# The third unit of each up projection waits for all four PSUM tiles of its opening

## What is computed

```
def swiglu_ffn(x, w_in, w_down):                      # layers 0 and 1
    h = x @ w_in                                      # 1024 -> 2 * 2816
    g, u = h[..., :FFN_HIDDEN], h[..., FFN_HIDDEN:]
    return (jax.nn.silu(g) * u) @ w_down

def _conv_ffn(h, w_up, conv_w, conv_b, w_down):       # second block
    a = h @ w_up
    ap = jnp.pad(a, ((0, 0), (CONV_W - 1, 0), (0, 0)))
    conv = conv_b + ap[:, 0:S] * conv_w[0]
    for j in range(1, CONV_W):
        conv = conv + ap[:, j:j + S] * conv_w[j]
    gate, val = jnp.split(conv, 2, axis=-1)
    return (jax.nn.silu(gate) * val) @ w_down
```

## Time and profile before

| | |
|---|---|
| median of 3 runs | 2296.75 us |
| all runs | 2290.5, 2296.75, 2320.01 us |
| span of the profiled execution | 2302.4 us |
| TensorE busy | 2235.3 us, 97% |
| VectorE busy | 1271.0 us, 55% |
| ScalarE busy | 936.0 us, 41% |
| mean granted TensorE clock | 0.994 of full |

### The profile page before, as it was taken

The page is one execution under the profiler, slowest core; times in us unless marked ns, Lnnn a source line. Parts: engine busy times, 40 slices in busy tenths (PEclk is TensorE's granted clock), DMA queues, the critical chain, the costliest instruction groups (busy, mean ns, idle before and its releaser), DMA issues.

```text
span 2302.4 us, 47528 instructions
## 1 busy us (share of the span) xinstructions
PE 2235.3 (97%) x18842; PEld 2140.7 (93%) x18846; DVE 1271.0 (55%) x2590; ACT 936.0 (41%) x1547; POOL 298.9 (13%) x318
## 2 busy tenths in 40 slices
PE   7999999999999999989999999999999998999998
PEld 7978999999999996978999999999989898999998
DVE  6477443665553256889463476554165655656513
ACT  4566354332222143478363252222144554444312
POOL 3000300200000052336120110000033002000001
PEclk9999999999999999999999999999999999999999
DMA  6333341255542221200252245553312202333221
GB/s 172 81 94 92 104 143 56 83 140 142 138 137 101 91 66 56 74 2 1 92 164 75 74 110 140 154 144 110 106 49 92 79 20 75 91 104 97 95 106 55
DMA packets 303947, 219.07 MB, mean 95 GB/s; under 512 B 34442, under 2 KB 290384, under 8 KB 303824
## 3 DMA queue, kind: packets, MB, share of 16 engines
q1 hardware_dynamic: 251856, 188.79, 27.4%
q10 hardware_dynamic: 50208, 25.69, 4.3%
q0 software_dynamic: 1760, 2.88, 0.4%
HBM read 207.58 MB, written 2.10 MB: 91 GB/s over the span
## 4 chain that ended last, share of the span: by engine, by line
PE 90%; ACT 4%; DVE 2%; POOL 2%; issue 1%; DMA 0%; DVEq 0%; SPq 0%; POOLq 0%; ACTq 0%
PE bank L714 69%; PE bank L831 5%; PE bank L940 4%; PE bank L910 2%; PE bank L1259 2%; PE bank L1039 1%; PE bank L1210 1%; PE bank L1108 1%; POOL ZS L2562 1%; PE bank L1100 1%; PE bank L1193 1%; ACT SQ L1559 1%; PE bank L1311 1%; ACT BI L1355 1%; POOL ZS L2531 1%
## 5 line engine op out<-in xcount | busy, mean ns | idle before, releaser
L714 PE MATMUL bank<-XH,WH 128*128 128x256 f32 (+1 forms) x3184 | 887.4, 279 | 6.2 <-DVE HF L2245 2.7
L714 PE MATMUL bank<-XH,WL 128*128 128x256 f32 (+1 forms) x3184 | 886.0, 278 | 0.0
L714 PE MATMUL bank<-XL,WH 128*128 128x256 f32 (+1 forms) x3184 | 886.0, 278 | 0.0
L681 DVE TENSOR_TENSOR WL<-RAW,WH 128x2048 fp32r<-128x2048 f32 x160 | 369.4, 2309 | 521.5 <-ACT WH L677 521.5
L714 PEld LDWEIGHTS bank<-XH,WH 128*128 128x128 f32 (+1 forms) x3184 | 599.0, 188 | 7.1 <-issue 4.1
L714 PEld LDWEIGHTS bank<-XH,WL 128*128 128x128 f32 (+1 forms) x3184 | 600.5, 189 | 0.0
L714 PEld LDWEIGHTS bank<-XL,WH 128*128 128x128 f32 (+1 forms) x3184 | 597.4, 188 | 0.2 <-issue 0.2
L677 ACT ACTIVATE WH<-RAW 128x2048 fp32r<-128x2048 f32 x171 | 327.5, 1915 | 584.1 <-PE bank L714 545.6
L714 PE MATMUL bank<-HH,WH 128*128 (+1 forms) x1056 | 293.4, 278 | 0.9 <-DVE HF L2245 0.9
L714 PE MATMUL bank<-HH,WL 128*128 (+1 forms) x1056 | 293.3, 278 | 0.0
L714 PE MATMUL bank<-HL,WH 128*128 (+1 forms) x1056 | 293.2, 278 | 0.0
(11 more groups left out here) (359 smaller groups left out, 3666.6 us busy)
## 6 DMA issues: line engine op xcount, KB each, us to landing
RAW<-in_ffn_w_in SPq DMA_DIRECT2D x88, 512.0 KB, 4.7
MB<-in_mod_w ACTq DMA_DIRECT2D x48, 512.0 KB, 5.0
RAW<-in_ffn_w_down SPq DMA_DIRECT2D x44, 512.0 KB, 4.0
RAW<-in_ffn_up SPq DMA_DIRECT2D x44, 512.0 KB, 4.6
RAW<-in_xa_w_kv SPq DMA_DIRECT2D x32, 512.0 KB, 4.4
RAW<-in_ffn_down SPq DMA_DIRECT2D x22, 512.0 KB, 3.9
RAW<-in_xa_w_q SPq DMA_DIRECT2D x16, 512.0 KB, 4.2
RAW<-in_xa_w_o SPq DMA_DIRECT2D x16, 512.0 KB, 4.0
```

What stands on the lines that cost most here:

```text
L681: nc.vector.tensor_tensor(WL[:, par, :], RAW[:, par, :], f32(WH[:, par, :]), ALU.subtract).then_inc(w_split, 1)
L714: mm = nc.tensor.matmul(out_ap[:, cols], l, moving, start=(start and n == 0 and k == 0), stop=(stop and n == len(parts) - 1 and k == len(o ...
```

## The change

One wait is added on TensorE, between the opening and the loop over the further units, in each stage that opens in halves and has more than two units. It lets TensorE go on when all four tiles of the opening have been read out of PSUM.

```
--- before.py
+++ after.py
@@ -762,6 +762,8 @@
                         behind(i, j)
                 if halves:
                     in_halves(name, xs, fill, amid)
+                    if UNITS[name] > 2:
+                        pe.wait_ge(tile_free, TILE0[name] + 4)
                     by_pairs(pe, UNITS[name] - 2, lambda i, j: unit(i + 2, j))
                 elif fill is None:
                     by_pairs(pe, UNITS[name], unit)
```

## The result

The changed kernel takes 2333.5 us (median of 4 runs, 2320.6 to 2342.0) against 2300.9 for the kernel before (4 runs, 2290.5 to 2320.0). The ratio is 1.0124, with a 95% interval of 1.0076 to 1.0173: slower by 1.2%, 29 us. The profiled execution took 2335.3 us and has a span of 2333.5. Some executions in the experiments have a mean granted clock of 0.97 in place of 0.99 and take some 30 to 50 us more; the ratios leave out every time over 1.5% above the fastest of its kernel, which is all but one of these and four at the full clock, two of them of the kernel with the wait in the second block alone.

A forecast was written before the change was run, and what follows sets the result against it. TensorE, busy 97% of a 2302.4 us span, was taken as the bound. Stops 22.0, restarts 0.6 and low clock 5.1 add 27.7 us to the median 2296.75, giving 2324, range 2306 to 2341.

The forecast's parts named there:

- The place and the count: Three waits, at the third units of ffn_in0, ffn_in1 and ffn_in2; TILE0 + 4 is reached only with the second unit's product.
- The stops: At the three third units TensorE waits for the second unit's product: 6.6, 6.9 and 8.5 us more, 22.0 in sum.
- The restart: Wait on the branch opening each loop keeps TensorE's queue from filling: 3 x 0.2 = 0.6 us.
- The rival of an instruction fetch: A fetch behind each of the three waits: 3.9 us instead of 0.6, time 2327.8; chance 0.07.
- The clock: Half speed for 3.4 us of matmuls behind each of three pauses: 3 x 1.7 = 5.1 us, between 0 and 10.2.
- prediction's signs of being wrong: Much smaller idle times, another stage moving more than spacing explains, or a clock low for far longer than 6.8 us.
- The spacing: Matmuls run at 117.8 or about 113.3 ns; the slower costs one feed-forward about 12.9 us, either sign.
- the forecast's assumption: As many slow stretches after the change as before, so spacing adds nothing to the sum; forecast's chance 0.35.
- Rival (a): The restart brings the fast spacing; the layer 0 stretch gains 12.9 us, giving 2311.5; chance 0.26.
- Rival (b): The restart brings slow spacing in the other two feed-forwards: one 2337.3, chance 0.15; both 2350.2, chance 0.06.
- The sum: Whole kernel: 22.0 + 0.6 + 5.1 = 27.7 us more, 2324.4 against the median 2296.75.

The follow-up runs named there:

- first-unit run: The changed kernel with its wait in the same place but asking for TILE0 + 1, the first unit's product, in place of TILE0 + 4; ratio to before 1.0025.
- filled pause: The changed kernel with 56, 56 and 96 matmuls of no use in the pauses ahead of the three waits; ratio to before 1.0138.

## Why the prediction was right

**The place and the count.** Three stops, each released by the second unit's product, at the two lines named. The first-unit run shows that the wait itself is free where it is met.

**The stops** were put at 6.6, 6.9 and 11.2 us, 22.0 more than before, with 0.6 for the restarts on top, and are 6.99, 6.77 and 11.47, 22.6 more, restarts included. Shown by the run that read the second unit first: the wait stayed and the stops went down to 1.83, 1.61 and 8.13.

**The restart** was taken at 0.24 us, the upper bound, 0.2 more than the 0.04 already counted, and measured 0.33, the same at all three: 0.9 us in place of 0.6 in sum. The rival of an instruction fetch (3.9 us) fell, as the first matmul came those 0.33 us behind the product. The Trainium skill's rule (Runtime: NRT & Kernel Launch, Instruction fetch mechanics) on taken branches did not bear on this loop.

**The clock**: 5.1 us supposed, 7.0 measured, within 0 to 10.2. The term was small because I took 3.4 us of matmuls at half speed behind each pause, as behind the 3 us pauses of the earlier trace rows, and these longer ones had 5, 5 and 3.5. One of the prediction's signs of being wrong was a clock low for far longer than 6.8 us: at the third place it was low for at least the 10 us shown, but it is the matmuls at half speed that cost, and of these there were 3.5 us. That the clock was the cause of those 7 us is shown by the filled pause, where all but 0.6 of them vanish. The Trainium skill (TensorE: Matmul & The Clock Gate, The HAM clock gate) calls the low clock the resting state that activity lifts. The trace agrees at the three pauses, where it goes from 1.00 to 0.50 and back to 1.00 behind 3.5 to 5 us of matmuls; the 96 us at half with TensorE 99% busy are not explained by it.

**The spacing** was the term of either sign, and the forecast's assumption, as many slow stretches after as before, is a statement on averages that a profile can't confirm: the two profiles of each kernel have different ones. What the runs confirm is that it is no property of the kernel, and that the times' spread comes from it: two profiles 13 us apart agree within 0.2 us without it. Rival (a), the fast spacing behind each pause, was wrong: layer 0 in the first profile of the changed kernel and layer 1 in the second were slow behind theirs. Rival (b) was wrong in the same way: neither is set. One step was incomplete: I treated a feed-forward as one stretch, but in the second block the down projection is dealt a spacing of its own, since TensorE stops ahead of it.

**The sum**: 27.7 us. Measured 29 by the ratio, 31.1 by the two spans, 30.9 without the spacings. The stops with their restarts were forecast at 22.6 and measured 22.6. The term that was too small is the clock at the three pauses, by 1.9 us. Of the other 1.3 us some 0.3 are still at these places, as the idle time is counted from a matmul's modelled end and not from where the next one would have begun (by the starts the first two third units come 7.15 and 6.93 us late). The rest is in stretches like the opening of `fox_u`. That the forecast's ratio, 1.0121, lies so near the measured 1.0124 is luck: the interval is half a per cent to each side, and one feed-forward more or less at the slow spacing is 0.6%.

## What to carry to other kernels

When an engine waits for a buffer to be read out, look at what stands ahead of the read-out in the reading engine's queue, and not at the read-out alone; here that was 5 of 7 us in two places, and putting the read-out first took it away. In the third, where the read-out itself is longer, it was 3.3 of 11.5 us. A long pause on the bounding engine is then paid a second time in the clock behind it, here with 1.7 to 2.8 us behind each pause of 6.8 to 11.5 us, and with nothing behind 1.6 and 1.8 us. And before a difference of 1% is put down to a change, see whether long even stretches run at the same pace in both profiles: here two executions of one program differ by 13 us for no reason in the code.

## What the runs showed of the hardware

- Streams of weight load and 256-column matmul, with nothing else in the way and the clock full, run at 113.3 or at 117.8 ns a matmul, and keep one for up to 342 us. Which one it is is settled at a break and differs between executions of one program. A one-pass matmul of 32 columns swaps the two, 60 times in a row; an fp32 one set the fast one in all up projections and not elsewhere. Six of them made this kernel 1.0% faster (0.66 to 1.3%). What the state is, I can't say. The Trainium skill (TensorE: Matmul & The Clock Gate, Back-to-back issue gap) gives N / 2.4 + 2.5 ns, 109.2 for 256 columns, for an isolated matmul; neither level is that. For a stream with weight loads it names no figure for 256 columns, but some 81 ns for 128 and 131 ns for 512, and both levels lie between these.
- At the third units the clock fell in every pause of 6.7 to 11.5 us, behind 1.6 and 1.8 us not, and behind about 3 us in some executions (at `ffn_in2`, 2.96 us in one profile and 2.43 in another, that of the small one-pass matmul: yes; 2.68 in the kernel before: no). So the length of such a short pause alone doesn't settle it.
- A wait on the jump that opens a loop cost nothing where it was met (0.12 us from matmul to matmul). Where TensorE stood at it, the first matmul came 0.33 us behind the releasing instruction's end, against 0.04 us where the wait was not on the jump.
- In two of fourteen profiles the clock stayed at half for 96 us in one piece, from 863 or 864 us on, with TensorE busy 99% of that time, which cost some 41 us.
